# The third weighted one-hot of each route group made on GpSimd in the V stage

## The reference, cut to what matters

```python
def block(xb):
    ...
    v1, i1 = lax.top_k(s1, PEER_TOPK)
    v2, i2 = lax.top_k(s2, PEER_TOPK)
    ...
    e = (jnp.take_along_axis(i1, ci // PEER_TOPK, axis=-1) * PEER_N_KEYS
         + jnp.take_along_axis(i2, ci % PEER_TOPK, axis=-1))
    g = jax.nn.softmax(cs.astype(jnp.float32), axis=-1)
    u = u_tab[e]
    a = jax.nn.gelu(jnp.einsum('pd,phkd->phk', xb, u).astype(jnp.float32), approximate=False)
    return jnp.einsum('phk,phkd->pd', g * a, v_tab[e].astype(jnp.float32)).astype(xb.dtype)
```

## Time and profile before

| | us |
|---|---|
| median of 3 runs | 2680.19 (2678.42 to 2687.99) |
| span of the profiled execution | 2678.9 |
| V stage of layer 0: first V matmul, last route group | 638.60, 843.08 |
| V stage of layer 1: first V matmul, last route group | 1617.24, 1821.52 |

### The profile page before, as it was taken

One profiled execution on the slowest core, in us unless ns is written; L12 is line 12 of the kernel. 1 busy time (PEld: TensorE's weight loads), 2 busy tenths in 40 slices (PEclk: granted clock), 3 DMA queues, 4 the chain that ended last, 5 costly groups with the idle time before them and its releaser, 6 DMA issues.

```text
span 2678.9 us, 49509 instructions
## 1 busy us (share of the span) xinstructions
PE 2576.6 (96%) x17564; PEld 2253.4 (84%) x17564; DVE 2112.4 (79%) x3580; ACT 1215.1 (45%) x1760; POOL 461.4 (17%) x369
## 2 busy tenths in 40 slices
PE   5999999999999999899999999999999999989998
PEld 4879999888877787899998888778878799767986
DVE  6787997888898768868978888997777877657754
ACT  3444445554434445444444454434445554324543
POOL 1104992000000000007990000000011000100000
PEclk8999999999999999899999999999999999999999
DMA  8754555555567877354555555577786556854454
GB/s 310 250 186 160 178 176 172 166 164 165 167 220 234 277 258 247 132 179 158 178 178 170 166 164 167 187 226 262 267 277 248 197 183 209 288 206 159 158 184 145
DMA packets 147692, 536.92 MB, mean 200 GB/s; under 512 B 16848, under 2 KB 17232, under 8 KB 147296
## 3 DMA queue, kind: packets, MB, share of 16 engines
q1 hardware_dynamic: 115088, 417.08, 46.6%
q0 software_dynamic: 31168, 113.26, 12.3%
q10 hardware_dynamic: 1296, 4.72, 0.5%
HBM read 531.85 MB, written 3.15 MB: 200 GB/s over the span
## 4 chain that ended last, share of the span: by engine, by line
PE 78%; DVE 9%; issue 4%; POOL 3%; DMA 2%; ACT 2%; DVEq 0%; ACTq 0%; POOLq 0%; SPq 0%
PE ps L1933 19%; PE ps L1504 9%; PE ps L716 7%; PE ps L2651 7%; PE ps L1478 6%; PE ps L1430 5%; PE ps L1508 5%; PE ps L2633 4%; PE ps L1482 3%; POOL split_lo L1555 3%; PE ps L1891 3%; PE ps L2637 2%; DVE split_lo L1567 2%; PE ps L369 1%; DVE mod_acc L406 1%
## 5 line engine op out<-in xcount | busy, mean ns | idle before, releaser
L1542 ACT ACTIVATE split_hi<-ring 128x1024 fp32r<-128x1024 f32 x764 | 805.4, 1056 | 770.5 <-PE ps L1482 202.0
L1567 DVE TENSOR_TENSOR split_lo<-ring,split_hi 128x1024 fp32r<-128x1024 f32 x576 | 702.3, 1220 | 202.2 <-ACT split_hi L1542 201.7
L1555 POOL TENSOR_TENSOR split_lo<-ring,split_hi 128x1024 fp32r<-128x1024 f32 x128 | 341.0, 2679 | 155.7 <-ACT split_hi L1542 155.3
L1539 ACT ACTIVATE gate_hi<-gate 128x256 fp32r x256 | 106.9, 418 | 441.5 <-PE ps L1933 441.5
L1933 PE MATMUL ps<-split_hi,gate_hi 128*128 128x512 f32 x1024 | 284.2, 398 | 0.5 <-ACT split_hi L1542 0.5
L1933 PE MATMUL ps<-split_hi,gate_lo 128*128 128x512 f32 x1024 | 276.6, 391 | 3.3 <-DVE gate_lo L1565 3.3
L1933 PE MATMUL ps<-split_lo,gate_hi 128*128 128x512 f32 x1024 | 276.8, 391 | 0.0
L1478 PE MATMUL ps<-h_parts,split_hi 128*128 128x256 f32 x2048 | 266.8, 283 | 0.0
L1504 PE MATMUL ps<-h_parts,split_hi 128*128 128x512 f32 x1024 | 261.2, 397 | 0.0
L1478 PEld LDWEIGHTS ps<-h_parts,split_hi 128*128 128x128 f32 x2048 | 254.9, 192 | 0.0
L386 POOL DMA_DIRECT2D mod_w<-in_mod x96 | 50.8, 529 | 1139.8 <-ACT gate L1608 418.3
(11 more groups left out here) (399 smaller groups left out, 4019.8 us busy)
## 6 DMA issues: line engine op xcount, KB each, us to landing
ring<-in_stream SPq DMA_DIRECT2D x782, 512.0 KB, 4.5
mod_w<-in_mod POOLq DMA_DIRECT2D x96, 512.0 KB, 4.8
small<-in_mod POOLq DMA_DIRECT2D x80, 512.0 KB, 6.0
gate<-in_mod POOLq DMA_DIRECT2D x32, 512.0 KB, 7.0
gate<-in_mod ACTq DMA_DIRECT2D x8, 512.0 KB, 11.6
gate<-in_mod SPq DMA_DIRECT2D x8, 512.0 KB, 10.3
x_kept<-x POOLq DMA_DIRECT2D x8, 256.0 KB, 3.9
gate<-x_kept POOLq DMA_DIRECT2D x4, 512.0 KB, 8.5
```

Source lines behind the costliest of these rows:

```text
L1542: nc.scalar.activation(split_hi[:, e, :], ring[:, slot, e * D:(e + 1) * D], ACT.Copy).then_inc(hi_made, 1)
L1555: nc.gpsimd.tensor_tensor(split_lo[:, e, :], ring[:, slot, e * D:(e + 1) * D], split_hi[:, e, :].bitcast(F32), ALU.subtract).then_inc(lo_m ...
L1567: nc.vector.tensor_tensor(split_lo[:, e, :], ring[:, (START[name] + j) % RING, e * D:(e + 1) * D], split_hi[:, e, :].bitcast(F32), ALU.sub ...
```

## The change

In the odd passes (V) three things are different. DVE writes `equal` into a buffer of its own, `equal_v`, which lies over `w_left` and is one buffer for all groups, so before writing it DVE waits until the previous group's products are done, its own (`hot_rows`) and POOL's (`hot_third`). DVE then makes two of the three weighted one-hots. POOL makes the third, `hot_r[r][2]`, in `hot_third_gpsimd`, once `equal` is there; PE waits for it too. The strip loads, which POOL used to issue as soon as a slot was free, are now put between the products of groups 2 to 31: the load with number n - 15 stands behind the product of group n (n = 17 to 31), and the rest follow after group 31. The even passes (u stages) are as before.

```diff
+            def load_when_used(i, k):
+                if l or not isinstance(i, int) or i or k >= 2:
+                    pool.wait_ge(mod_used, i * DC + (l * LOOP_STRIPS * DC + k - 1))
+                load(i, k)
+
+            def hot_third_gpsimd(n):
+                pool.wait_ge(hot_equal, (2 * l + 1) * GROUPS + n + 1)
+                nc.gpsimd.tensor_tensor(pairs(hot_r[n % 2][2]), pairs(equal_v), of_token(4, HALF, n // 8, n % 8),
+                                        ALU.mult).then_inc(hot_third, 1)
+            hot_third_gpsimd(0)
+            hot_third_gpsimd(1)
             pool.wait_ge(u_drained, (l + 1) * 68)
-            for k in range(DC):
-                if l or k >= 2:
-                    pool.wait_ge(mod_used, l * LOOP_STRIPS * DC + k - 1)
-                load(0, k)
-            with pool.Fori(1, LOOP_STRIPS) as i:
+            load_when_used(0, 0)
+            load_when_used(0, 1)
+            for n in range(2, 32):
+                hot_third_gpsimd(n)
+                if n > 16:
+                    load_when_used((n - 15) // DC, (n - 15) % DC)
+            for m in range(17, 3 * DC):
+                load_when_used(m // DC, m % DC)
+            with pool.Fori(3, LOOP_STRIPS) as i:
                 for k in range(DC):
-                    pool.wait_ge(mod_used, i * DC + (l * LOOP_STRIPS * DC + k - 1))
-                    load(i, k)
+                    load_when_used(i, k)
...
+        equal_v = w_left.bitcast(BF16).rearrange("p (a b) -> p a b", a=GROUP)
...
-            equal = pairs(hot_r[r][0])
-            nc.vector.tensor_tensor(equal, of_key((p % 2) * HALF, HALF), of_token(0, HALF),
+            odd = p % 2
+            equal = pairs(equal_v if odd else hot_r[r][0])
+            if odd:
+                v.eng.wait_ge(hot_rows, i * 8 + (p * GROUPS + j))
+            if odd and not (first and j == 0):
+                v.eng.wait_ge(hot_third, i * 8 + (p // 2 * GROUPS + j))
+            elif odd and p > 1:
+                v.eng.wait_ge(hot_third, p // 2 * GROUPS)
+            nc.vector.tensor_tensor(equal, of_key((p % 2) * HALF, HALF), of_token(0, HALF, i, j),
                                     ALU.is_equal).then_inc(hot_equal, 1)
...
-            for m in reversed(range(W_PARTS)):
-                ins = nc.vector.tensor_tensor(pairs(hot_r[r][m]), equal, of_token(2 + m, HALF), ALU.mult)
+            for m in reversed(range(W_PARTS - odd)):
+                ins = nc.vector.tensor_tensor(pairs(hot_r[r][m]), equal, of_token(2 + m, HALF, i, j), ALU.mult)
             ins.then_inc(hot_rows, 1)
...
                     if routes:
+                        t.eng.wait_ge(hot_third, i * 8 + (l * GROUPS + j + 1))
                         routes_group_tensor(t, i * 8 + ((2 * l + 1) * GROUPS + j), j % 2)
```

More of the change, by code:

```diff
@@ L260, in build @@
         hot_equal = sem("hot_equal")
+        hot_third = sem("hot_third")
         mlp_drained, mlp_squared, hid_made = sem("mlp_drained"), sem("mlp_squared"), sem("hid_made")
@@ L1770, in at, with pairs, of_key, of_token @@
             return ap2d[:, bass.ds(i * step + off, n)]
+        def pairs(ap):
+            return ap.rearrange("p t (k q) -> p t k q", q=PAIR)
+        def of_key(k0, n):
+            return keys_bf[:, k0:k0 + n].rearrange("p (k q) -> p k q", q=PAIR).unsqueeze(1) \
+                .to_broadcast([P, GROUP, n // PAIR, PAIR])
+        def of_token(m, n, i, j):
+            if isinstance(i, int):
+                ap = selT[:, m, 64 * i + 8 * j:64 * i + 8 * j + 8, :]
+            else:
+                ap = selT[:, m, bass.ds(i * 64 + 8 * j, 8), :]
+            return ap.unsqueeze(2).to_broadcast([P, GROUP, n // PAIR, PAIR])
         def routes_group_vector(v, p, i, j, first):
@@ L1778, in routes_group_vector @@
                 v.eng.wait_ge(routes_full, i * 8 + (p * GROUPS + j - 1))
[L1779 to L1791, removed]
-            equal = pairs(hot_r[r][0])
-            nc.vector.tensor_tensor(equal, of_key((p % 2) * HALF, HALF), of_token(0, HALF),
+            odd = p % 2
[7 more added lines that the diff above has]
+            nc.vector.tensor_tensor(equal, of_key((p % 2) * HALF, HALF), of_token(0, HALF, i, j),
                                     ALU.is_equal).then_inc(hot_equal, 1)
-            nc.vector.tensor_tensor(pairs(hot_c[r]), of_key(0, KEYS), of_token(1, KEYS),
+            nc.vector.tensor_tensor(pairs(hot_c[r]), of_key(0, KEYS), of_token(1, KEYS, i, j),
                                     ALU.is_equal).then_inc(hot_cols, 1)
             v.eng.wait_ge(hot_equal, i * 8 + (p * GROUPS + j + 1))
-            for m in reversed(range(W_PARTS)):
-                ins = nc.vector.tensor_tensor(pairs(hot_r[r][m]), equal, of_token(2 + m, HALF), ALU.mult)
+            for m in reversed(range(W_PARTS - odd)):
+                ins = nc.vector.tensor_tensor(pairs(hot_r[r][m]), equal, of_token(2 + m, HALF, i, j), ALU.mult)
             ins.then_inc(hot_rows, 1)
```

## The result

The changed kernel takes 2740.86 us in the median of 4 runs (2719.94 to 2745.18), the kernel before 2679.74 us (now 4 runs, 2678.42 to 2687.99): the ratio is 1.0211, with a 95% interval of 1.0185 to 1.0237. By the medians it is slower by 61 us, by the ratio by 57, since one of the four runs is 18 us under the others. The forecast was 2716 (2696 to 2755).

What follows compares the result with a forecast made beforehand. PE bounds the kernel, except 28 slab periods of V set by DVE. Hold 23.5, first slabs 2.5 and loads 10 make +36 us on the 2680.19 us median: 2716 us, range 2696 to 2755.

Steps and rivals of the forecast that it cites:

- Ceiling and gain of the removed product: V's 28 DVE-set slab periods: at most 16.9 us from relieving DVE; one product fewer gives 9.3 us before costs.
- POOL and DVE exclude each other for two SBUF inputs: V's slabs: POOL's product and DVE's two-SBUF-input instructions do not run side by side; DVE stands for POOL's whole length.
- Rival D: V's products: POOL runs beside DVE without slowing it; 2690 us, within 0.5% of before; chance 0.06.
- The hold: DVE standing for POOL's product in V: 1.17 us, net +0.84 a slab, 23.5 us over 28 DVE-set periods.
- its neighbours: Cases near the sum: DVE held 0.9 to 1.5 us, loads 0 to 22 us; 2697 to 2745 us, chance 0.66.
- The first slabs: First 16 slabs of each V, no strips: DVE slightly over PE's 6.29 us; 32 slabs cost 1 to 4, taken 2.5.
- The loads: Strip loads queued behind POOL's products: DVE waits 0.83 us for them 12 times in V, 10 us.
- rival C: Strip loads land in time, under 3.9 us after issue: 2706 us; its chance lies inside the first case's 0.66.
- POOL goes in between two DVE instructions that were ready: V's route group: POOL's product gets its turn when DVE's column comparison ends, ahead of DVE's two products.
- wherever POOL's falls, DVE pays for it: V's slabs: every DVE instruction but the merge has two SBUF inputs, so DVE pays except where already waiting.
- PE waiting on POOL and not on DVE: Sign of a wrong prediction in V's profile: POOL goes after DVE's products; no size given.
- POOL goes before DVE's two products, so DVE ends last and the wait adds nothing of its own: PE's added wait for `hot_third` in V: put at nothing, since DVE's products would end after POOL's.

Runs made afterwards that it cites:

- no_third2: The changed kernel without POOL's product, PE reading the second one-hot twice in V, loads alone on POOL's queue: 2673.64 us, 0.9978 of the kernel before.
- under_merge: The changed kernel with DVE's comparison for the next group made ahead of the merge, so POOL wakes during the merge: 2683.58 us, 1.0013 of the kernel before.
- two_products: wait_third2 with POOL's product made twice into the same place, DVE and PE waiting for the second: 2763.21 us, 1.0325 of the kernel before.
- wait_third2: The changed kernel plus a DVE wait for POOL's product right behind DVE's own two products: 2702.98 us, 1.0094 of the kernel before.
- loads_early2: The changed kernel with strip loads 6 to 9 and 14 to 17 one product earlier on POOL's queue: 2728.66 us, 1.0196 of the kernel before.

## Why the prediction came out as it did

The sign and the range were right, the range in part by luck, as the sum at the end shows; the forecast of +36 us met +61.

- *Ceiling and gain of the removed product.* Right. 9.3 us forecast for the relief without a product on POOL, 6.6 measured (no_third2).
- *POOL and DVE exclude each other for two SBUF inputs.* Right, read from the earlier trace rows, and shown by under_merge and two_products. Rival D falls: DVE's products are longer while POOL is active, 1.53 us for 0.67.
- *The hold.* Mis-sized: 1.17 us forecast, 0.86 measured, under even the 0.9 to 1.5 that the forecast gave its neighbours. The estimate took half of the fp32 split's. In a slab with a chunk the net is 0.53 and not 0.84, 28 x 0.53 = 15 us and not 23.5. The first slabs cost 0.04 us each, 32 x 0.04 = 1.3, against 2.5. That leaves wait_third2, at +23, some 7 us above the sum. Its 18 short lost races, at 0.44 us each, make 8 of them (an estimate from the rows above); the forecast had none.
- *The loads.* Wrong as put: 12 waits of 0.83 us were forecast, and wait_third2, which has the loads in the same place, waits for them no longer than the kernel before (11.7 us in all, 11.5 before). In its blocks the loads landed 3.7 us after their issue in the median (3.5 to 5.0), where I took 4.7, so the condition of rival C held; and a product that is not held up ends 0.3 us earlier than I took.
- *"POOL goes in between two DVE instructions that were ready", and "wherever POOL's falls, DVE pays for it", no more.* This is the step that failed. The earlier trace rows show two turns of POOL, both won, and I made a rule of them. In 11 of 28 slabs with DVE as the bound DVE's product was first, and then nothing lets POOL in for 3 to 5 us. Then DVE does not pay, PE does, and the strip load, and the clock. I had named the mark of it, PE waiting on POOL and not on DVE, among the signs of a wrong prediction, without a price. In the sum this was a term put at nothing: "POOL goes before DVE's two products, so DVE ends last and the wait adds nothing of its own". The wait was 32.9 us in 11 slabs of the profile, and with what came behind it its price is 2741 - 2703 = 38 us.

So the terms for the hold and for the loads were too high by about 10 us each, and the lost races were missing: 8 us for the short ones and 38 for the long. 36 - 20 + 46 = 62, against 61 measured. The result was inside the range in part by luck, because these errors were of opposite sign.

Of the 38 us, loads_early2 gives up to 12 back by better-placed loads. The rest is PE's waiting (32.9 us in the profile, partly covered) and the clock. They were not separated.

## What to carry to other kernels

Moving an elementwise instruction from DVE to POOL was no relief here, where DVE's neighbours have two SBUF inputs: DVE stands for POOL's whole turn (0.86 us here, for 0.33 saved), so place it under a DVE instruction that reads PSUM, or leave it. If POOL's result is waited for, make DVE wait too, which took 38 us of the loss away here: a DVE that never idles can keep POOL out for many instructions, and whoever waits for POOL, and whatever is queued behind it, pays. A cost that one trace shows twice is not a rule about who goes first; look for what would happen if the order turned.

## What the runs showed of the hardware that was not expected

- POOL's product of 128x512 bf16 takes 1.03 us undisturbed and holds DVE up for 0.86; the 128x1024 fp32 split takes 2.43 and holds it up for 2.24.
- The time at which POOL asks does not settle who goes first: asking 0.16 to 0.19 us after the start of the same DVE instruction, it got in between in one slab (1.43 us) and stood in another (5.02 us).
- PE's idle stretches of 2.50 and 4.39 us before the route groups at 750.95 and 786.49 were followed by slower matmuls (1.43 and 1.44 us for what takes 0.87); one of 1.60 us at the double chunk in the kernel before was not (0.87). The length alone does not decide it: in the changed kernel two waits of 2.54 us for DVE's products came before the groups at 767.78 and 838.14, and the first was followed by slower matmuls (1.26), the second not (0.87).
